# Adding the causal mask on DVE, in PSUM, in place of an identity matmul: a forgetting-attention pipeline on one core

## What is computed

```python
def _fox_attend(q, k, v, cq, ck, qpos, kpos):
    s = jnp.einsum('bngqd,bnkd->bngqk', q, k).astype(jnp.float32) * (DH_B ** -0.5)
    s = s + cq[..., :, None] - ck[..., None, :]
    s = jnp.where(kpos[None, :] <= qpos[:, None], s, NEG)
    p = jax.nn.softmax(s, axis=-1)
    return jnp.einsum('bngqk,bnkd->bngqd', p.astype(v.dtype), v)
```

## Time and profile before

| | |
|---|---|
| median of 3 runs | 3288.41 us (3288.33 to 3294.2) |
| profiled execution | 3289.06 us, of which the trace spans 3287.2 |
| granted TensorE clock, mean | 0.978 |
| PE busy / PEld busy | 3080.2 us (94%) / 2950.0 us (90%) |
| DVE / ACT / POOL busy | 2014.2 (61%) / 1125.2 (34%) / 994.3 us (30%) |
| layer 1's attention pipeline | from 1825 to 2220 us of the span |

### The profile page before, as it was taken

The page is one execution under the profiler, slowest core; times in us unless marked ns, Lnnn a source line. Parts: engine busy times, 40 slices in busy tenths (PEclk is TensorE's granted clock), DMA queues, the critical chain, the costliest instruction groups (busy, mean ns, idle before and its releaser), DMA issues.

```text
span 3287.2 us, 49995 instructions
## 1 busy us (share of the span) xinstructions
PE 3080.2 (94%) x18927; PEld 2950.0 (90%) x18927; DVE 2014.2 (61%) x3240; ACT 1125.2 (34%) x2381; POOL 994.3 (30%) x591
## 2 busy tenths in 40 slices
PE   6899999898999999999987999999999999999997
PEld 5888888797999999999977888889799999999997
DVE  4666565526565666556776677772666656556775
ACT  4454555403222222222431566651422222222242
POOL 2122222231222222222333787763122222212231
PEclk8999999899999999999998999999999999999998
DMA  3112221411111111111103211131111111111111
GB/s 120 55 59 67 65 68 56 140 39 33 46 45 45 46 45 45 45 39 53 42 19 103 62 55 53 57 122 45 33 46 45 45 40 46 43 45 45 53 40 61
DMA packets 254712, 181.60 MB, mean 55 GB/s; under 512 B 26868, under 2 KB 237508, under 8 KB 254404
## 3 DMA queue, kind: packets, MB, share of 16 engines
q1 hardware_dynamic: 239576, 163.53, 16.6%
q10 hardware_dynamic: 14956, 15.54, 1.5%
HBM read 142.54 MB, written 36.50 MB: 54 GB/s over the span
## 4 chain that ended last, share of the span: by engine, by line
PE 74%; DVE 11%; issue 6%; ACT 5%; DMA 2%; POOL 1%; SPq 0%; ACTq 0%; DVEq 0%; POOLq 0%
PE ps L951 22%; PE ps L953 21%; PE ps L952 21%; ACT t L1579 2%; PE ps L1248 2%; PE ps L1116 2%; PE ps L1052 1%; PE ps L1069 1%; PE ps L1136 1%; DMA t<-in_w_qkv_a 1%; DVE t L2073 1%; DVE t L1996 1%; DVE t L1917 1%; ACT t L1635 1%; DVE t L1904 1%
## 5 line engine op out<-in xcount | busy, mean ns | idle before, releaser
L951 PE MATMUL ps<-t,t 128*128 128x384 f32 (+1 forms) x4920 | 1651.1, 336 | 60.8 <-DVE t L1956 11.5
L953 PE MATMUL ps<-t,t 128*128 128x384 f32 (+1 forms) x4920 | 1616.2, 329 | 0.0
L952 PE MATMUL ps<-t,t 128*128 128x384 f32 (+1 forms) x4920 | 1614.9, 328 | 0.0
L951 PEld LDWEIGHTS ps<-t,t 128*128 128x128 f32 x4920 | 931.9, 189 | 110.0 <-DVE t L1904 31.4
L952 PEld LDWEIGHTS ps<-t,t 128*128 128x128 f32 x4920 | 932.5, 190 | 0.2
L953 PEld LDWEIGHTS ps<-t,t 128*128 128x128 f32 x4920 | 931.1, 189 | 0.0
L770 POOL TENSOR_TENSOR t<-t,t 128x1024 fp32r<-128x1024 f32 x181 | 478.1, 2642 | 1254.2 <-ACT t L1687 1250.9
L1878 DVE TENSOR_TENSOR t<-t,ps 128x384 f32<-128x384 f32 x528 | 261.9, 524 | 158.4 <-PE ps L953 156.4
L2168 DVE TENSOR_SCALAR t<-t 128x2 f32 (+1 forms) x88 | 16.8, 190 | 435.5 <-ACT t L1713 435.5
L1687 ACT ACTIVATE t<-t 128x1024 fp32r<-128x1024 f32 x130 | 138.0, 1062 | 410.7 <-PE ps L953 410.7
L1701 ACT ACTIVATE t<-ps 128x384 f32<-128x384 f32 x176 | 86.5, 492 | 499.6 <-PE ps L953 499.6
(11 more groups left out here) (162 smaller groups left out, 3380.7 us busy)
## 6 DMA issues: line engine op xcount, KB each, us to landing
t<-in_w_ffn_in SPq DMA_DIRECT2D x88, 512.0 KB, 3.8
t<-in_w_ffn_out SPq DMA_DIRECT2D x44, 512.0 KB, 3.3
t<-in_w_qkv_a SPq DMA_DIRECT2D x24, 512.0 KB, 4.0
t<-in_w_ple_gate SPq DMA_DIRECT2D x16, 512.0 KB, 3.8
out<-t SPq DMA_DIRECT2D x32, 192.0 KB, 2.1
t<-in_w_o_a SPq DMA_DIRECT2D x8, 512.0 KB, 4.1
t<-in_w_q_b SPq DMA_DIRECT2D x8, 512.0 KB, 4.6
t<-in_w_o_b SPq DMA_DIRECT2D x8, 512.0 KB, 4.0
```

The costliest lines, as they stand in the source:

```text
L951: pe.matmul(out, a_hi, b_hi, start=start, stop=False, skip_group_check=True)
L952: pe.matmul(out, a_hi, b_lo, start=False, stop=False, skip_group_check=True)
L953: return pe.matmul(out, a_lo, b_hi, start=False, stop=stop, skip_group_check=True)
```

## The change

`scores_b` no longer runs the identity matmul; the last gates matmul of the map signals `s_done`. `maximum_b` first adds the mask tile onto the last 128 (or 64) columns in PSUM, and signals a new semaphore, for which the reduction waits. Nothing else is moved, and no buffer changes.

```diff
-                    pe.matmul(out, q_pick[:, m, a:b], k_gates[:, first + c0:first + c1], start=False, stop=c1 < width,
-                              skip_group_check=True)
-                w = 128 if t < 8 else TS
-                pe.matmul(psf[:, 1024 * m + width - w:1024 * m + width], ident_r[:, :], causal_r[:, P - w:P], start=False,
-                          stop=True, skip_group_check=True).then_inc(s_done, 1)
+                    mm = pe.matmul(out, q_pick[:, m, a:b], k_gates[:, first + c0:first + c1], start=False, stop=True,
+                                   skip_group_check=True)
+                mm.then_inc(s_done, 1)
...
             def maximum_b(n, m):
                 col = 2 * (n % 2) + m
                 dve.wait_ge(s_done, scored(n, m))
+                w, width = 128 if n % 9 < 8 else TS, width_b(n)
+                last = psf[:, 1024 * m + width - w:1024 * m + width]
+                dve.tensor_tensor(last, last, causal_r[:, P - w:P].bitcast(F32), ALU.add).then_inc(causal_added, 1)
+                dve.wait_ge(causal_added, 2 * n + m + 1)
                 dve.tensor_reduce(negmax[:, col:col + 1], psf[:, 1024 * m:1024 * m + width_b(n)], AX.X, ALU.max,
                                   negate=True).then_inc(max_done, 1)
```

More of the change, by code:

```diff
@@ L414, in program @@
         scaled0, scaled1 = sem("scaled0"), sem("scaled1")
+        causal_added = sem("causal_added")
         early_done, early_added = sem("early_done"), sem("early_added")
```

## The result

| | before | changed |
|---|---|---|
| median | 3288.5 us (3284.61 to 3294.46, 6 runs) | 3304.03 us (3302.85 to 3305.75, 6 runs) |
| profiled execution | 3289.06 us, span 3287.2 | 3304.21 us, span 3302.4 |
| granted clock, mean | 0.978 | 0.976 |

The ratio is 1.0045, with an interval of 1.0032 to 1.0057: the changed kernel is slower by 0.45%. The forecast was 3302 us.

What follows compares the result with a forecast made beforehand. No engine was taken as full: PE works in bursts between answers from ACT and DVE. Units sum 1.02 + 3 x 1.94 + 3 x 2.16 + 0.13 = 13.5 us; from 3289.06, median 0.65 lower: 3302 us, range 3291 to 3311.

Steps and rivals of the forecast that it cites:

- The bound: In the pipeline, no engine is full; PE works in bursts between answers from ACT and DVE.
- The slot of an identity: PE time until the next matmul starts: 0.11 us per identity, 15.9 us for 144 if all counted.
- the walk: Tile-by-tile delay of PE's next start through a unit: 2.16 us in units 2, 4, 6; 1.94 in 1, 3, 5.
- The addition, 0.29 + 0.04: On DVE, 128 columns take 294 ns plus a 0.04 us wait, so a reduction ends 0.33 us later.
- The bounds of 0.20 and 0.45: Cheapest and dearest delay per DVE addition, in us; the whole some 6 us (3295) or 22 us (3310).
- what PE saves in four maps goes into that 0.92: Tiles 2 to 4, even unit: PE's savings vanish in its 0.92 us wait for POOL before tile 5's transposes; +0.33.
- 0.33 - 0.22 = +0.11: Tiles 2 to 4, odd unit: POOL's run starts a tile later, behind two saved identities, so +0.11 us.
- First and last unit: Unit 0, starting without backlog, ends at +1.02 us; the last, with a transfer wait at tile 3, at +0.13.
- The sum: All units' delays together: 13.5 us, handed on whole through the later stages.
- PE is the bound: Rival: PE's saved time counts everywhere in the pipeline, 15.9 us faster, 3272.5 us; chance 0.06.
- The chain stays: Rival: a unit pays three maxima, gains eleven identities: about -0.3 us, 3286; chance 0.14, shared with additions cheaper than 0.20.
- All in series: Rival: all 144 additions delay the pipeline one after another, +47 us, 3336; anything above 22 us had chance 0.05.

Runs made afterwards that it cites:

- the last experiment: Before kernel, tile 1's output sum first, DVE masking only last unit's tiles 2 to 6 and map 0 of tiles 7, 8: 3283.79 us, ratio 0.9978.
- map 0 alone: Before kernel with DVE adding the mask for map 0 of each tile, map 1 keeping its identity matmul: 3294.4 us, ratio 1.0011.
- adding twice: Changed kernel with two mask additions per map on DVE, each with its wait: 3328.82 us in its one execution.

## Why the prediction was right

**The bound.** It said that no engine is full and that PE works in bursts between answers. Removing 15.9 us of PE's time gave back 5.15, with nothing added. Right.

**The slot of an identity, 0.11 us.** No run measured it apart from the rest. Of the 108 x 0.11 = 11.9 us in units 1 to 6 the walk had let 2.0 count (0.22 in an even unit, 0.44 in an odd one). Measured are 2.4, by the kernel that adds and keeps the identity, and 3.57 where nothing is added. So the small share was right.

**The addition, 0.29 + 0.04.** It is 0.294, with a gap of 0.03 behind it. The bounds of 0.20 and 0.45 were not needed, and PE's writes into PSUM beside it did not make it dearer.

**The walk.** In unit 2, as predicted and as measured, by how much later they come than before: values of tile 0 +0.40 and +0.41; POOL at tile 2 +1.06 and +1.07; transposes of tile 5 +1.06 and +1.05; start of tile 7 +1.73 and +1.75; start of tile 8 +1.98 and +1.98; the whole unit 2.16 and 2.15. The step "what PE saves in four maps goes into that 0.92" held too: that wait is still 0.92.

**Odd units.** Here the size was off. The prediction had them at 1.94, with two saved identities ahead of POOL's start; they grew by 2.03, 2.08 and 2.03. The term "0.33 - 0.22 = +0.11" is the one in which they differ from even units, and its 0.22 did not give back too much. The kernel that adds and keeps the identities grew by 2.51, 2.60 and 2.54 in odd units and by 2.46, 2.39 and 2.44 in even ones, where the walk has 2.38 for both. So the identities gave back about 0.5 in an odd unit (0.44 predicted) and 0.3 in an even one (0.22), and it is the additions of an odd unit that cost about 0.17 more than the walk has. That is there by the start of tile 7 (in unit 1, 1.92 against 1.73); which of the steps up to tile 6 it belongs to is not shown.

**First and last unit.** Predicted +1.02 and +0.13, measured +1.10 and +0.21. The last is uncertain by about 1 us, since its wait for the transfer differs between traces: 0.33 us before, none after, 1.07 in the last experiment, 1.50 with map 0 alone.

**The sum.** 13.5 predicted, 13.88 in the pipeline. The medians differ by 15.5, more than that; the 1.6 us between lie within what the stages outside, which have no edit, do from execution to execution (6 us ahead at one place, 2 us lost behind the pipeline).

**The rivals.** *PE is the bound* (-15.9) falls by the kernel that only removes: -5.15. *The chain stays* (-0.3 a unit) falls by the walk: all four more additions were on the path. It also had eleven identities on the chain give 1.2 us a unit, and without any addition a unit gave only 0.6. *All in series* (+47) falls by the same trace; adding twice shows how it would be approached, with twelve of eighteen on the path. The rule of the Trainium skill ("Perfetto Trace Analysis", section "Identifying the Most-Contended Engine"), to optimize the engine with the highest occupancy first, points to TensorE here. By the measurements its load had little to give, and moving work off it to the less busy VectorE cost 13.9 us.

**What did fail** are three expectations of experiments. That the sum ahead of the maximum would free tile 0 of its 0.3 us left out what stands behind it on DVE. That the sum ahead of the maximum in the kernel before would give 0.4 us in tile 1 counted the whole time by which the sum starts sooner, where PE's wait for it was 0.35 in unit 2; it gave 0.31 there and 0.18 in odd units. And that full PE in the last unit would turn its saved identities into time left out the wait for the transfer at tile 3: it grew by 0.74 us, 0.33 of it because PE came earlier. It does not account for all that was missing.

## What to carry to other kernels

Where engines answer each other in a tight round, the busiest engine's load is not the price of its work: ask of each instruction moved who waits for what stands *behind* it in the list of the engine that gets it. The same exchange of a matmul for an addition cost 0.27 us a unit for one map and 1.5 for the other. A short instruction is free only ahead of one that waits for something else; count that slack once, since two additions that share it pay for it together. And where an edit is worth less than the drift of the stages around it, read it from a fixed stretch of the trace, not from the whole time.

## What the runs showed of the hardware

- DVE's addition in place in PSUM takes 294 ns for 128 columns next to PE's matmuls into other banks, the same as in layer 0, and 222 for 64.
- An instruction of DVE that waits for the one before it starts 0.03 us behind its end (the reduction at 1918.09 behind the addition that ends at 1918.06); without the wait it may start 0.08 us ahead of it (the reciprocal at 1918.30, the reduction's end at 1918.38).
- Stages with the same instructions differ by several us between two executions (4 to 6 us ahead at one place, 1 us at the next). Part of it goes with the granted clock: of 30 executions of the kernel before, the five with a mean clock of 0.979 took 3287.1 us on average and the five with 0.976 took 3292.8, and in the pipeline the clock was 1.00 in every trace, so this lies in the other stages. The times within one value of the clock still differ by up to 10 us, and no run here shows why.
